# Sparse attention of a two-block network: fixed score and turn banks, values ahead of turning, copies ahead of exponentials and scaling

## The reference, cut to what matters

```python
sc = einsum('bhgqd,bhnd->bhgqn', qn, k_cmp) * scale        # 15 compressed keys
pc = _masked_softmax(sc, cmp_end[None, :] <= t_pos[:, None])
o_c = einsum('bhgqn,bhnd->bhgqd', pc, v_cmp)
ps = _masked_softmax(ss * scale, ms)                       # selected keys
pw = _masked_softmax(sw * scale, mw)                       # window keys
return gt[..., 0:1] * o_c + gt[..., 1:2] * o_s + gt[..., 2:3] * o_w
```

## Time and profile before

| | |
|---|---|
| median of 3 runs | 2070.7 us |
| lowest, highest | 2059.89, 2072.95 us |
| span of the profiled execution | 2057.3 us |
| instructions | 32710 |
| busy: PE, DVE, ACT, POOL | 94%, 66%, 52%, 12% |
| mean granted TensorE clock | 0.969 |

### The profile page before, as it was taken

One profiled execution on the slowest core, in us unless ns is written; L12 is line 12 of the kernel. 1 busy time (PEld: TensorE's weight loads), 2 busy tenths in 40 slices (PEclk: granted clock), 3 DMA queues, 4 the chain that ended last, 5 costly groups with the idle time before them and its releaser, 6 DMA issues.

```text
span 2057.3 us, 32710 instructions
## 1 busy us (share of the span) xinstructions
PE 1936.8 (94%) x13400; PEld 1652.7 (80%) x13400; DVE 1349.8 (66%) x2060; ACT 1073.3 (52%) x1744; POOL 248.5 (12%) x267
## 2 busy tenths in 40 slices
PE   5999989999999899899999889999988899999998
PEld 3775668888787785899998888999877688888886
DVE  4348546767545658678566556545665788888887
ACT  3346524333334466566555425445445577676774
POOL 1101121111100100222112412111113000000000
PEclk9999999999999999999999999999999899999999
DMA  8423343455322220245553113555542489889794
GB/s 323 161 105 123 144 175 130 169 186 180 118 80 89 91 100 22 99 169 193 213 183 130 41 43 121 199 185 205 205 164 87 188 323 344 310 330 344 307 351 162
DMA packets 52812, 364.81 MB, mean 177 GB/s; under 512 B 5936, under 2 KB 8240, under 8 KB 8880
## 3 DMA queue, kind: packets, MB, share of 16 engines
q1 hardware_dynamic: 50304, 359.68, 47.2%
q10 hardware_dynamic: 2352, 2.96, 0.5%
HBM read 361.57 MB, written 1.05 MB: 176 GB/s over the span
## 4 chain that ended last, share of the span: by engine, by line
PE 82%; DVE 9%; ACT 4%; issue 3%; POOL 1%; DMA 1%; SPq 0%; DVEq 0%; POOLq 0%; ACTq 0%
PE ps L77 22%; PE ps L78 21%; PE ps L79 21%; PE ps L74 15%; DVE WLO L91 2%; PE ps L82 2%; ACT R L85 2%; ACT WHI L85 1%; DVE SM L105 1%; POOL R L91 1%; DVE R L91 1%; DMA ring<-W 1%; DVE HLO L88 1%; DVE h L88 1%; DVE x L88 0%
## 5 line engine op out<-in xcount | busy, mean ns | idle before, releaser
L91 DVE TENSOR_TENSOR WLO<-ring,WHI 128x1024 fp32r<-128x1024 f32 x562 | 676.3, 1238 | 181.1 <-ACT WHI L85 180.2
L85 ACT ACTIVATE WHI<-ring 128x1024 fp32r<-128x1024 f32 x566 | 577.6, 1052 | 89.4 <-PE ps L79 85.5
L77 PE MATMUL ps<-HHI,WHI 128*128 128x256 f32 (+1 forms) x1584 | 512.9, 324 | 28.5 <-DVE HLO L88 18.6
L78 PE MATMUL ps<-HLO,WHI 128*128 128x256 f32 (+1 forms) x1648 | 524.5, 318 | 0.0
L79 PE MATMUL ps<-HHI,WLO 128*128 128x256 f32 (+1 forms) x1584 | 506.2, 320 | 0.0
L77 PEld LDWEIGHTS ps<-HHI,WHI 128*128 128x128 f32 x1584 | 303.9, 192 | 71.1 <-issue 32.0
L78 PEld LDWEIGHTS ps<-HLO,WHI 128*128 128x128 f32 x1648 | 316.0, 192 | 22.7
L79 PEld LDWEIGHTS ps<-HHI,WLO 128*128 128x128 f32 x1584 | 303.6, 192 | 23.9
L74 PE MATMUL ps<-R 64*64 64x64 f32 (+10 forms) x2448 | 192.5, 292 | 5.3 <-ACT R L85 3.2
L85 ACT ACTIVATE R<-ps,VEC 128x512 f32<-128x512 f32 (+1 forms) x106 | 69.1, 658 | 237.4 <-PE ps L79 235.6
L91 POOL TENSOR_TENSOR R<-R 128x256 f32<-128x256 f32 (+1 forms) x99 | 108.3, 1098 | 547.5 <-ACT R L85 546.3
(11 more groups left out here) (222 smaller groups left out, 2983.9 us busy)
## 6 DMA issues: line engine op xcount, KB each, us to landing
ring<-W SPq DMA_DIRECT2D x340, 1024.0 KB, 4.9
x<-xt SPq DMA_DIRECT2D x2, 1024.0 KB, 6.4
out<-x SPq DMA_DIRECT2D x2, 512.0 KB, 4.8
CR<-const_nsa ACTq DMA_DIRECT2D x1, 560.0 KB, 3.8
CR<-const_rw ACTq DMA_DIRECT2D x1, 448.0 KB, 3.4
CR<-const_gqa ACTq DMA_DIRECT2D x1, 320.0 KB, 9.7
CR<-const_mla ACTq DMA_DIRECT2D x1, 320.0 KB, 2.8
VEC<-vec ACTq DMA_DIRECT2D x1, 314.0 KB, 10.9
```

The source lines that it names most:

```text
L77: self.e.matmul(out, l[0], r[0], start=start, stop=False)
L78: self.e.matmul(out, l[0], r[1], start=False, stop=False)
L85: return self.e.activation(out, in_, func, **kw)
L91: return self.e.tensor_tensor(out, in0, in1, op)
```

## The change

Three things change, all in the sparse attention.

Banks: at the scores of step 0 four banks are taken out of the rotation and kept as `nS`; step i uses the two of its tile. At the start of `nsa_pe` two more are taken as `nT`, one for each turned half. The pairs' outputs take from the remaining two. All go back to the list at the end.

PE's order: the values of step i-2 are issued before the turning of step i-1.

ACT's and DVE's order: both put their copy of turned weights (step i-2) earlier, ACT ahead of the exponentials of step i (and the output of a finished pair ahead of that), DVE ahead of the normalisation of step i-1.

```diff
+        return take_at(pe, label, freed, i)
+
+    def take_at(pe, label, freed, i):
         if i in freed_by:
             pe.wait_ge(*at(*freed_by[i]))
...
-        bs = [take(pe, ("nS", i, z), ("nexpz", i, z)) for z in range(2)]
+        if i == 0:
+            nS.extend(turn_of.pop(0) for _ in range(4))
+        bs = [take_at(pe, ("nS", i, z), ("nexpz", i, z), nS[2 * tile + z]) for z in range(2)]
...
-            b = take(pe, ("nT", i, half), ("npt", i, half))
+            b = take_at(pe, ("nT", i, half), ("npt", i, half), nT[half])
...
     def nsa_pe(pe):
+        nT.extend(turn_of.pop(0) for _ in range(2))
         for i in range(1, 10):
             if i < 7:
                 nsa_scores_pe(pe, i + 1)
+            if i >= 2:
+                nsa_values_pe(pe, i - 2)
             if 1 <= i <= 8:
                 nsa_turn_pe(pe, i - 1)
-            if i >= 2:
-                nsa_values_pe(pe, i - 2)
+        turn_of[:0] = nS
+        turn_of.extend(nT)
     def nsa_act(a):
         for i in range(11):
+            if i >= 4 and i % 2 == 0:
+                nsa_out_act(a, i // 2 - 2)
+            if 2 <= i < 10:
+                nsa_copy(a, i - 2, 1)
             if 1 <= i < 8:
                 nsa_exp_act(a, i)
             if 2 <= i < 6:
                 hi_units(a, L["o_out"].first[i - 2:i - 1])
-            if 2 <= i < 10:
-                nsa_copy(a, i - 2, 1)
-            if i >= 4 and i % 2 == 0:
-                nsa_out_act(a, i // 2 - 2)
     def nsa_dve(v):
...
                 nsa_max_dve(v, i)
+            if i >= 2:
+                nsa_copy(v, i - 2, 0)
             if 2 <= i <= 8:
                 nsa_normalise_dve(v, i - 1)
-            if i >= 2:
-                nsa_copy(v, i - 2, 0)
```

More of the change, by code:

```diff
@@ L3196, in nsa_copy @@
         t.then_inc(*did("turned_act" if half else "turned_dve", ("npt", i, half)))
-    nO = [None]
+    nO, nS, nT = [None], [], []
     def nsa_values_pe(pe, i):
```

## The result

The changed kernel is slower by a third of a per cent: 2070.15 us median of 20 runs (2064.79 to 2082.82) against 2063.86 us median of 20 runs before (2057.99 to 2108.72), ratio 1.0036 with a 95% interval of 1.0024 to 1.0048, or +7.4 us (5.0 to 9.9); the medians themselves differ by 6.3. That is inside the range and inside the 1% that I called no change, on the side that was forecast, and more than twice the +3.1 us of the sum. The median of before over 20 runs is 6.8 us lower than that of the three runs shown ahead.

What follows compares the result with a forecast made beforehand. PE dominates the chain of waits (82%); in the sparse attention a DVE-PE cycle of maxima, multiplication and turning binds. Terms 1.2 + 3.0 - 1.3 + 0.2 = +3.1 us on the 2070.7 median gave 2073.8 us, range 2060 to 2080.

Steps and rivals of the forecast that it cites:

- the sum: All terms of the forecast over the sparse attention added up: +3.1 us, bounds -1 to +6.
- the ring: Sparse attention's limiting cycle: DVE's maxima, small DVE operations ending in a multiplication, PE's turning, maxima again; copies and values outside.
- Banks at 0: Kept score and turn banks: step 3's wait stays, turn banks freed by copies a loop step earlier; 0 us.
- Values of step 0 in front, +1.2: PE, step 0's values before step 1's turning: delays turning and maxima, net +1.2 us, bounds 0.4 to 2.2.
- DVE's copy, 0.60 each, and POOL's stalls: DVE: copy paid in loop steps 3 to 7, +3.0 us; shorter stalls behind POOL -1.3, step 6 +0.2.
- Cover of the values in mid-stretch: PE, later steps: values fit before DVE's multiplication ends, 0 us; at the lower clock 0.3 to 0.4 stick out.
- The tail at 0: Pipeline's end: step 6's values +0.3 us, one step's values fewer behind the last turning gives 0.3 back; 0.
- the copies' term: DVE's copy entering the cycle of waits in loop steps 3 to 7: 5 x 0.60 = +3.0 us.
- Nothing behind the stretch: After the sparse attention: weight loads and DMA untouched, output projection's banks in another order but all free; no cost.
- the clock rival: Turnings of steps 2 to 6 all at the lower clock: +7.7 us, 2078.4 us; chance 0.13, including 0.03 long form.

Runs made afterwards that it cites:

- e1: Kernel before with the kept banks alone, all three orders as before: sparse-attention stretch 40.8 us against 39.7 before, ratio 1.0008.
- e8: The changed kernel run again, unchanged, for the spread: stretch 46.2 us against 44.6 in its first profile, ratio 1.0028 against the kernel before.
- e5: The changed kernel with 28 extra matmuls that nobody reads where PE idles: stretch 40.5 us against 44.6, ratio 0.9998 against the kernel before.
- e9: Kernel before with kept banks, all orders as before, and 17 extra matmuls that nobody reads where PE idles: stretch 38.2 us, ratio 1.0005.
- e3: Kernel before with DVE's order alone changed (copy ahead of normalisation): stretch 40.0 us against 39.7 before, ratio 1.0005.
- e2: Kernel before with ACT's order alone changed (output and copy ahead of the exponentials): stretch 42.7 us against 39.7 before, ratio 0.9999.
- e10: Kernel before without DVE's small scaling by 0.125, queries scaled in ACT's copy instead: stretch 35.9 us against 39.7 before, ratio 0.9987.

## Why the prediction was right or wrong

The call was right: the change is slower by an amount under 1%, for want of anything in the ring that it shortens. The size was not: the change cost 7.4 us and the sum says 3.1. The total of 2073.8 us is within 4 us of the measured 2070.15 by luck, since the three runs that it starts from lie 6.8 us above the median of twenty. Taken by its steps:

- **Banks at 0.** Right for the change as made, but the reason given was not. The copies that free the turn banks do not run a loop step earlier; they run in the same one (the copy of step i-2 in the loop step of the turning of step i-1), and are early only because they stand ahead of the normalisation. e1 has them behind it, and its turnings wait for them.
- **Values of step 0 in front, +1.2.** The first profile has +0.4, the second +2.1 (maxima of step 3 at 9.2 and 10.9 against 8.8 us). The bounds were 0.4 and 2.2, and which end comes up is the clock's.
- **DVE's copy, 0.60 each, and POOL's stalls.** The copy is there at 0.59 or 0.60 in each chain row. The scaling of steps 4, 5 and 6 took 0.17, 0.24 and 0.42 us in the first profile and 0.60, 0.36 and 0.72 in the second. Less its own 0.17, that is stalls of 0, 0.07 and 0.25, and of 0.43, 0.19 and 0.55; forecast were 0.35, 0.2 and 0.2 more at step 6. From the maxima of step 3 to those of step 7 it makes 21.8 us in one and 21.8 in the other, against 20.7: +1.1, where these terms summed to 1.9 less the copy of step 7, 1.3.
- **Cover of the values in mid-stretch.** Held but for one turning: those of steps 2, 4, 5 and 6 wait 0.26 to 0.86 us for the multiplication, and that of step 3 stood behind late values for some 0.15 us. DVE's wait for turning was forecast at 1.2 us and was 1.25 to 2.12.
- **The tail at 0.** This step failed. The tail grew by 3.4 us in both profiles (13.6 against 10.2 us), of which 0.6 is the copy of step 7 that the copies' term had, so 2.8 were not foreseen. I worked it with a slow turning and values at 1.24, at the higher clock. In fact values, turning and values run at the lower level, 2.17, 1.97 and 1.98, and both values stand behind a wait of 0.8 us for ACT's copy. Before, the last turning ran at 1.09, and all 28 matmuls of the last two values behind it took 2.1 us together. Filled, the tail took 10.0 us.
- **Nothing behind the stretch.** The second failure: the lower level reaches into the output projection for +1.5 us (11.7 against 10.2), as it did in e8 (11.9); filled it was 10.6. A further +1.2 follows in the router, in the first pair only; in e8 that part was 0.8 shorter than before, so I don't count it to the change.

So the mechanism was right and the rest was the clock rival in small: I gave it 0.13 as an alternative to the sum, with turnings of steps 2 to 6 as its place. It belonged into the sum, in the tail, where PE has the least work. The rule that the forecast cited beside that rival (the Trainium skill, "TensorE: Matmul & The Clock Gate", section "HAM oscillation — how this bites in real kernels", on loops whose waits recur) spoke for what happened in the tail, where the granted clock was 0.50 between the waits.

Open stays how much of the loss the order alone costs at one clock. Before with its rotation and filled, but with the scaling, was not run. From the kernel before, less the 2.3 us at step 3 and 0.9, 0.8 and 0.8 for the slow turnings and last values, I estimate 35 us against e5's 40.5, of which 1.4 are slow scores at step 3: some 4 us, near the 1.2 + 3.0 of the sum without what POOL gives back. That is worked out, not shown. How it divides between banks and orders is open as well: e9 has kept banks, the old orders and a fill, and took 38.2 us, against 40.5 less 1.4 for e5, so by this estimate the orders cost about 1 us where the banks are kept, and the rest would go with the banks.

## What to carry to other kernels

In a ring of three engines, first ask of each moved piece whether it was in the shadow of another; the copy on DVE was, and moving it ahead put 0.6 us into each step, part of which shorter stalls behind POOL gave back. When banks are fixed, list for each bank who frees it and where that stands in its engine's order: here two turn banks and two late copies cost 2 to 3 us that a rotation had hidden. And price the thin end of a pipeline at the lower clock if waits there come between short pieces of PE's work: an order that only adds waits of 0.8 us nearly doubled the time of everything between them.

## What the runs showed of the hardware that was not expected

Matmuls that nobody reads can pay: 28 of them shortened a stretch of 44.6 to 46.2 us to 40.5, with every turning at 1.09 us, and the median of the whole by 7.3 us.

The work of PE in the stretch did not fix when the clock rose. With the same PE work and the same 4.0 us wait ahead of it, the higher level came back some 5 to 6 us after that wait in the kernel before (turning 1.97, then values 1.50 and scores at full speed), in e3 before the first turning (1.09), and in e2 only after 13 us of unbroken work (granted clock 0.50 from 1538.74 to 1551.70 us), the turning of step 2 still at 1.97. Repeats of one kernel agreed for before and differed by 1.7 us for the changed one. A difference of 2 us between two profiles of such a stretch is no evidence until the turnings' times are compared.

A DVE operation on 128x4 elements took several times as long when one of POOL's subtractions was under way: the scaling 1.19 for 0.17 us (before) and 2.10 (e2), and the form with two SBUF inputs 0.79 for 0.16 (e10); 128x1024 took 1.71 for 1.23. The rule that the prediction cites (the Trainium skill, "SBUF — State Buffer", section "Who interferes with whom") says so of both forms, and the ends of the longest stalls agree with POOL's to 0.02 or 0.03 us.
